# Third feed-forward: gate and up units streamed as pairs of 256 and 512 columns instead of triples of 256

## What is computed

```python
h = rmsnorm_2(x, norm_ffn[l])
ug = causal_dwconv(h @ w_ffn_in[l], conv_w[l], conv_b[l])   # 3 taps along the tokens
u, g = jnp.split(ug, 2, axis=-1)
x = x + (jax.nn.silu(g) * u) @ w_ffn_out[l]
...
return rmsnorm_2(x, norm_final)
```

## Time and profile before

| | |
|---|---|
| median of 3 runs | 923.34 us (923.24 to 924.99) |
| the profiled execution, its time | 923.12 us |
| its span in the trace | 921.3 us |
| TensorE busy | 887.1 us (96%) |
| DVE busy | 651.3 us (71%) |
| ACT busy | 435.9 us (47%) |
| third feed-forward, G1 to the end of D10 | about 736 to 912 us |
| mean granted TensorE clock | 0.983 |

### The profile page before, as it was taken

How to read it: one execution, slowest core, us unless ns; L and a number is a source line. 1 busy time by engine, 2 the same in 40 slices (tenths; PEclk the granted TensorE clock), 3 DMA queues, 4 the chain that set the end, 5 groups by cost and what they waited for, 6 DMA issues and landing times.

```text
span 921.3 us, 14268 instructions
## 1 busy us (share of the span) xinstructions
PE 887.1 (96%) x5595; PEld 792.9 (86%) x5602; DVE 651.3 (71%) x832; ACT 435.9 (47%) x544; POOL 38.8 (4%) x38
## 2 busy tenths in 40 slices
PE   4999999999999799999999999999999999999995
PEld 3988888888899688888888889998988899999994
DVE  3577757667776677767666876757877788878776
ACT  4254444445234345444444545566534565555552
POOL 0000000000331200000000200200000000000000
PEclk8799999999999989999999999999999999999998
DMA  9365655554652745664656475533744447465441
GB/s 264 143 212 182 205 191 180 187 180 136 195 173 92 246 141 184 198 212 158 206 183 168 107 183 119 139 119 92 228 138 154 143 164 241 166 204 197 153 152 46
DMA packets 117886, 156.13 MB, mean 169 GB/s; under 512 B 3933, under 2 KB 103309, under 8 KB 117725
## 3 DMA queue, kind: packets, MB, share of 16 engines
q1 hardware_dynamic: 116236, 150.88, 52.1%
q0 software_dynamic: 768, 2.82, 0.9%
q10 hardware_dynamic: 848, 1.97, 0.6%
HBM read 154.59 MB, written 1.07 MB: 169 GB/s over the span
## 4 chain that ended last, share of the span: by engine, by line
PE 85%; DVE 8%; DMA 3%; ACT 3%; issue 1%; SPq 0%; DVEq 0%; ACTq 0%
PE wk L1373 30%; PE acc L1460 20%; PE wk L1398 17%; PE wk L1396 9%; DVE w_lo L775 3%; DMA raw<-in_ffn_w 2%; ACT w_hi L414 1%; PE wk L1689 1%; PE acc L1661 1%; PE acc L1540 1%; PE acc L1674 1%; DMA raw<-in_w_in 1%; PE acc L1410 1%; DVE xhl L786 1%; PE acc L1664 1%
## 5 line engine op out<-in xcount | busy, mean ns | idle before, releaser
L1373 PE MATMUL wk<-xhl,w_hi 128*128 128x256 f32 x1472 | 273.0, 287 | 2.0 <-DVE arena L1081 1.7
L1398 PE MATMUL wk<-xhl,w_hi 128*128 128x512 f32 x704 | 253.0, 402 | 0.0
L781 DVE TENSOR_TENSOR w_lo<-raw,w_hi 128x2048 fp32r<-128x2048 f32 x83 | 190.1, 2290 | 81.2 <-ACT w_hi L421 81.0
L1373 PEld LDWEIGHTS wk<-xhl,w_hi 128*128 128x128 f32 x1472 | 230.3, 192 | 6.9 <-issue 4.9
L1396 PE MATMUL wk<-xhl,w_lo 128*128 128x256 f32 x704 | 200.5, 285 | 9.6 <-DVE xhl L786 9.6
L1373 PE MATMUL wk<-xhl,w_lo 128*128 128x256 f32 x736 | 208.1, 283 | 0.0
L421 ACT ACTIVATE w_hi<-raw 128x2048 fp32r<-128x2048 f32 x83 | 157.9, 1904 | 27.0 <-PE wk L1373 27.0
L1398 PEld LDWEIGHTS wk<-xhl,w_hi 128*128 128x128 f32 x704 | 134.5, 191 | 32.6
L775 DVE TENSOR_TENSOR w_lo<-raw,w_hi 128x2048 fp32r<-128x2048 f32 x58 | 134.4, 2324 | 30.5 <-ACT w_hi L414 30.2
L1460 PE MATMUL acc<-w_hi,hhl 128*128 128x512 f32 x480 | 153.4, 391 | 0.0
L1396 PEld LDWEIGHTS wk<-xhl,w_lo 128*128 128x128 f32 x704 | 135.4, 192 | 12.0 <-issue 11.2
(11 more groups left out here) (245 smaller groups left out, 929.8 us busy)
## 6 DMA issues: line engine op xcount, KB each, us to landing
raw<-in_ffn_w SPq DMA_DIRECT2D x66, 1024.0 KB, 5.3
raw<-in_w_in SPq DMA_DIRECT2D x26, 1024.0 KB, 6.7
raw<-in_w_ffn_in SPq DMA_DIRECT2D x22, 1024.0 KB, 5.1
raw<-in_w_ffn_out SPq DMA_DIRECT2D x11, 1024.0 KB, 4.9
raw<-in_w_out SPq DMA_DIRECT2D x8, 1024.0 KB, 4.9
arena<-bias_scratch POOLq DMA_DIRECT2D x1, 2048.0 KB, 11.4
raw<-in_cmp_w_k SPq DMA_DIRECT2D x2, 1024.0 KB, 5.3
raw<-in_cmp_w_v SPq DMA_DIRECT2D x2, 1024.0 KB, 5.3
```

What stands on the lines that cost most here:

```text
L781: nc.vector.tensor_tensor(w_lo[:, s], raw[:, s], w_hi[:, s].bitcast(F32), ALU.subtract) \
L1373: mm = nc.tensor.matmul(dst, w, v, start=start and n == 0, stop=stop and n == len(pairs) - 1, skip_group_check=True)
L1398: return nc.tensor.matmul(bank, wh[:, c, cols], xhl[:, c].rearrange("p n t -> p (n t)"), start=False, stop=c == DC - 1, skip_group_check=True)
```

## The change

For the third feed-forward `parted` becomes true as well. Its gate and up units are made by `split_tile` (its first unit by `split_chunk`), so the gate takes banks 0 and 1 of `wk` and up banks 2 and 3. ACT gets two more instructions a step: a copy of the right halves of the gate's banks to `part3`, ahead of the high half of G(i+1), and one of up's, behind the tanh. Both wait for the unit, and for the DVE's last add out of `part3`. `scaled` on the DVE waits for ACT's copy instead of the unit, adds the two halves, and then multiplies in place. TensorE now waits for `a_sum` and `b_sum` before G and U, and, ahead of opening `acc`, for the copy of the reciprocal root mean square, which is now spread in bank 0 of `acc` and no more in bank 3 of `wk`.

```diff
--- before.py
+++ after.py
@@ -232,6 +232,7 @@
         conv_a, conv_b, t3_s, h3_s = (work[:, n] for n in range(2, 6))
         out_s = carve(0, 2, D)
         xf = sqf.rearrange("p (t d) -> p t d", t=2)
+        part3 = sqf[:, 0:2 * T]
         scratch = nc.dram_tensor("bias_scratch", (16, BIASW), F32, kind="Internal").ap()
 
         def x_bank(b):
@@ -661,13 +662,20 @@
                     hi_in_loop(i, U_FFN3, 1)
                 else:
                     hi(U_FFN3 + 2)
-                if isinstance(i, int) and i == 0:
+                first = isinstance(i, int) and i == 0
+                act.wait_ge(unit_done, U_FFN3 + 1 if first else i * 3 + U_FFN3)
+                act.wait_ge(b_sum, i + n0)
+                nc.scalar.activation(k_n(part3, 2), wk[:, 0:2, T:2 * T], ACT.Copy).then_inc(a_low, 1)
+                if first:
                     hi(U_FFN3 + 3)
                 else:
                     hi_in_loop(i, U_FFN3, 2)
                 conv_start(i, 0, a_s, conv_a, 22, a_out)
                 act.wait_ge(conv_2, i * 4 + 2)
                 nc.scalar.activation(t3_s, conv_a, ACT.Tanh, scale=0.5).then_inc(tanh_out, 1)
+                act.wait_ge(unit_done, U_FFN3 + 2 if first else i * 3 + (U_FFN3 + 1))
+                act.wait_ge(a_sum, i + (n0 + 1))
+                nc.scalar.activation(k_n(part3, 2), wk[:, 2:4, T:2 * T], ACT.Copy).then_inc(b_low, 1)
                 conv_start(i, 1, b_s, conv_b, 0, b_out)
                 if not (isinstance(i, int) and i == 0) and not last:
                     hi_in_loop(i, U_FFN3, 3)
@@ -1299,9 +1307,12 @@
             lo(U_FFN3 + 1)
 
 
-            def scaled(i, bank, dst, unit_end, out_sem):
-                dve.wait_ge(unit_done, unit_end)
-                nc.vector.tensor_tensor(k_n(dst, 2), halves(bank), bcast(rstd_b[:], 2), ALU.mult).then_inc(out_sem, 1)
+            def scaled(i, banks, dst, low_sem, sum_sem, out_sem):
+                dve.wait_ge(low_sem, i + (2 * FI + 1))
+                nc.vector.tensor_tensor(k_n(dst, 2), wk[:, banks:banks + 2, 0:T], k_n(part3, 2), ALU.add) \
+                    .then_inc(sum_sem, 1)
+                dve.wait_ge(sum_sem, i + (2 * FI + 1))
+                nc.vector.tensor_tensor(k_n(dst, 2), k_n(dst, 2), bcast(rstd_b[:], 2), ALU.mult).then_inc(out_sem, 1)
                 dve.wait_ge(out_sem, i + (2 * FI + 1))
 
             def taps(i, n, src, dst, f0):
@@ -1321,16 +1332,16 @@
                 if first:
                     rstd_diag(4)
                     lo(base + 2)
-                    rstd_copy(4, wk[:, 3, T:2 * T])
+                    rstd_copy(4, acc[:, 0, 0:T])
                 else:
                     lo_in_loop(i, base, 1)
-                scaled(i, wk[:, 0], a_s, base + 1 if first else i * 3 + base, a_out)
+                scaled(i, 0, a_s, a_low, a_sum, a_out)
                 if first:
                     lo(base + 3)
                 else:
                     lo_in_loop(i, base, 2)
                 taps(i, 0, a_s, conv_a, 22)
-                scaled(i, wk[:, 1], b_s, base + 2 if first else i * 3 + (base + 1), b_out)
+                scaled(i, 2, b_s, b_low, b_sum, b_out)
                 dve.wait_ge(tanh_out, i + (n0 + 1))
                 nc.vector.scalar_tensor_tensor(out=conv_a, in0=t3_s, scalar=1.0, in1=conv_a, op0=ALU.add,
                                                op1=ALU.mult).then_inc(h1_out, 1)
@@ -1476,7 +1487,7 @@
                 n0 = FI * f
                 s0, s1, s2 = base % SLOTS, (base + 1) % SLOTS, (base + 2) % SLOTS
 
-                parted = f < 2
+                parted = True
 
                 def col_unit(slot, j):
```

## The result

The changed kernel takes 931.25 us (median of 4 runs, 931.06 to 932.00), the kernel before 923.31: a ratio of 1.0083, with a 95% interval of 1.0066 to 1.0101. It is slower by 7.9 us, inside the predicted range and 2.2 us above the predicted time.

What follows compares the result with a forecast made beforehand. TensorE was taken to bound the loop, the ACT-DVE chain both ends of the third feed-forward. Start less loop savings +3.5 and end +2.4 gave +5.9 on 923.12: 929.0 us, own range 927.4 to 930.6, eight-in-ten range 926.2 to 932.0.

Steps and rivals of the forecast that it cites:

- the clock rival: TensorE's granted clock falls after a pause; first swallowed by the second, later ones not: 931 to 933 us, chance 0.13.
- the clock row dips behind a pause: Sign of being wrong in the next profile: granted clock falling after one of TensorE's pauses; no size given.
- The pairs' 0.19 us a step: TensorE's gate and up matmuls: fewer instructions for the same columns save 0.19 us a step, bounds nothing to about 0.4.
- The up part: Up's ACT-DVE chain each step: add 2.86 us after the gate's taps start instead of 1.57; 1.89 more in sum.
- The first pause: TensorE before the first down unit: waits about 2.9 us for the low part of its split.
- The second pause: TensorE before step 2's up unit: waits 2.4 us; that unit starts 4.9 us later than before.
- No stall in the loop: Later steps: ACT-DVE chain of 16.3 us a step stays shorter than TensorE's 16.79, so TensorE stalls no more.
- The end: From the end of step 10's gate unit to the last down unit: grows by 2.4 us, with a third pause.
- After D10 nothing changes: From the last down unit onward: no added time.
- the faster one: Added work stays covered at both ends and ten blocks give 0.19 us each: 921.2 us, chance 0.06.
- The one in which U2 doesn't pause: Step 1's chain overlaps more, so step 2's up unit does not wait: 926.6 us, chance 0.11.
- The one with the chain as the loop's bound: ACT-DVE chain reaches 17.1 us a step, each of eight steps adding 0.3: 931.4 us, chance 0.11.

Runs made afterwards that it cites:

- e1: Changed kernel without ACT's copies and the DVE's adds, only the paired streams kept; ratio 0.9982 to the kernel before, 921.6 us.
- e4: Changed kernel with ACT's copy of up moved ahead of its tanh; ratio 1.0023 to the kernel before.
- e10: The changed kernel as it is, profiled once more; one execution, 931.49 us.
- e5: Changed kernel with the change in steps 0 to 9 only, step 10 back to triples without copies or adds; ratio 1.0039, 926.9 us.
- e2: Kernel before, with its triples, plus ACT's copies and the DVE's adds in every step; ratio 1.0091, 931.7 us.
- e3: Changed kernel with 11 unused matmuls of 512 columns filling the pause before the last down unit; ratio 1.0063 to the kernel before.
- e6: Changed kernel with the change in steps 3 to 10 only, steps 0 to 2 back to triples without copies or adds; ratio 1.0024, 925.5 us.

## Why the prediction was right, and by how much it was off

The three pauses came at the places named, and D0, U2 and D10 are late by what was forecast, within 0.1 us. The forecast of 929.0 with its own range of 927.4 to 930.6 did not hold, though: 931.25 lies above it, where the clock rival (931 to 933) has its place. The wide range holds because it was drawn to take in most of that rival. One of my signs of being wrong, that the clock row dips behind a pause, came true.

- **The pairs' 0.19 us a step**: right, 16.79 in the changed kernel and in e1, which is 0.19 / 32 = 5.9 ns for each matmul saved. The Trainium skill ("TensorE: Matmul & The Clock Gate", section "Back-to-back issue gap") gives 2.5 ns beyond the columns for an isolated matmul; 0.08 us a step is an estimate from it. The trace of this stream doesn't bear that figure out.
- **The up part**: 2.86 from taps to add forecast, 2.84 measured; the multiply 0.73 later. e4 shows that the place behind the tanh is the larger half of it.
- **The first pause**: 2.9 forecast, 2.87 and 2.77 measured. D0 starts 750.68 - 731.42 = 19.26 us after the copy into `rstd_t`, 2.72 more than before; 2.71 was forecast.
- **The second pause**: 2.4 forecast; 2.23 measured where the clock held, 0.84 where D0 ran slower. That the one swallows the other stood in the clock rival, and e10 shows it. U2 starts 32.87 us after the copy into `rstd_t`, where it started 758.91 - 731.01 = 27.90 after it before: 4.97 late, 4.9 was forecast.
- **No stall in the loop**: right, but with less room: the chain is 16.41 a step, not 16.3, since the 0.13 that was taken off for the tanh did not come.
- **The end**: +2.4 forecast, counted from the end of G10. From the start of D9 to D10 it is 2.52 more; U10, which lies between G10 and D9, is 0.1 shorter now, so 2.4 measured; e5, which has the slower triples back in step 10, shows 2.30. The pause was 2.63, not 2.8.
- **"After D10 nothing changes"**: this step failed. The granted clock falls in D10, after the pause, and D10 and its tail last 1.65 longer. I had it as a rival with a chance of 0.13 because my pauses were shorter than the one of 3.37 us in the earlier trace rows. That comparison was worth little: e4 shows a fall after 1.79 us. With 1.65 for this term in place of 0, 929.0 becomes 930.7; 0.4 us more came from the stages ahead, which is what executions differ by.

Of the rivals, the faster one fails by e2 and e5: the added work is covered at neither end. The one in which U2 doesn't pause fails by U2's start, 4.97 late. The one with the chain as the loop's bound fails by the steps of 16.79.

## What to carry to other kernels

Before adding work to an engine that is far from full (the DVE was busy 13.44 of 16.98 us here), find the edges of its stage. In the middle of this loop 2.7 us of chain cost nothing; in the first two steps and the last one they cost nearly all they had, and the steps between could only give back 0.19 each. A gain that is paid per step belongs in the steps with slack: the same change in steps 3 to 9 is 0.17% faster, in all steps 0.83% slower. And where a copy goes into an in-order queue behind an instruction that waits, it inherits that wait: look at what stands ahead of it before looking at how long it is.

## What I had not expected of the hardware

The granted clock follows idle stretches less strictly than I thought. It was low after TensorE's pauses before D0 of 1.79 us (e4, 0.58 in the next stretch), 2.56 (e2, 0.79) and 2.87 (0.57 in the changed kernel, 0.80 in e3, 0.85 in e5). It stayed at 1.00 after pauses of 1.36 (e4, before D10), 2.23 (e10, before U2), 2.56 (e2, before D10) and 2.77 (e10, before D0). So a pause of the same 2.56 us had either outcome within one execution of e2. Before D10, the pause of 2.63 was followed by a low clock in three profiled executions of three (changed kernel, e6, e10). What decides it besides the length of the pause was not tried.
